# Seven small reorderings and shorter norms in a two-block f32 transformer kernel, with the identity products behind the expert loop taken out

## The reference

```python
def first_block(x, mem, ...):
    h = rmsnorm(x, g_mix)
    proj = h @ w_in                                  # q, k, v, u
    mixed = concat([rmsnorm(sb, g_sb_out), rmsnorm(pooled, g_pool_out)])
    x = x + mixed @ w_out
    x = x + memory_cross_attention(rmsnorm(x, g_mem_q), rmsnorm(mem, g_mem_kv), w_mem_q, w_mem_kv, w_mem_o)
    x = x + moe_ffn(rmsnorm(x, g_ffn), w_router, b_router, w1, b1, w2, b2)   # top 4 of 32, clamped SwiGLU
    return rmsnorm(x, g_final)

def second_block(x, p, ...):
    cols = _rms_norm(x, g_pre) @ w_in                # 1024 -> 6272 columns
    y_a, y_b = attention(...), time_mix(...)
    merged = sigmoid(gate_a) * (y_a @ p_a) + sigmoid(gate_b) * (y_b @ p_b)
    h = x + _rms_norm(merged @ w_out, g_post)
    return h + sigmoid(h @ w_ple_gate) * (p @ w_ple_up)
```

## Time and profile before

| | us |
|---|---|
| median of 3 runs | 1480.3 (1479.57 to 1480.72) |
| the profiled execution | 1479.94 |
| its span, first to last instruction | 1478.1 |
| TensorE busy | 1416.4 (96%) |
| VectorE, ScalarE, GpSimd busy | 485.1, 387.6, 72.0 |
| mean granted clock of TensorE | 0.995 |
| read from HBM | 479.2 MB |

### The profile page before, as it was taken

The page is one execution under the profiler, slowest core; times in us unless marked ns, Lnnn a source line. Parts: engine busy times, 40 slices in busy tenths (PEclk is TensorE's granted clock), DMA queues, the critical chain, the costliest instruction groups (busy, mean ns, idle before and its releaser), DMA issues.

```text
span 1478.1 us, 21334 instructions
## 1 busy us (share of the span) xinstructions
PE 1416.4 (96%) x9123; PEld 765.5 (52%) x9123; DVE 485.1 (33%) x736; ACT 387.6 (26%) x540; POOL 72.0 (5%) x74
## 2 busy tenths in 40 slices
PE   8999999999999999999999999999999899899997
PEld 8898984333333333333333333233333699888686
DVE  5475543112112112111211111112111467875465
ACT  6555532111111111111111111111111556631133
POOL 1220000000000000000000000000000100261000
PEclk9999999999999999999999999999999999999999
DMA  9545378999999999999999999999999545322332
GB/s 362 176 136 164 121 290 352 430 426 428 428 427 429 429 428 428 429 428 430 428 427 430 428 430 427 426 429 428 427 427 426 179 158 194 115 88 88 119 128 96
DMA packets 52532, 481.83 MB, mean 326 GB/s; under 512 B 4784, under 2 KB 10416, under 8 KB 27760
## 3 DMA queue, kind: packets, MB, share of 16 engines
q1 hardware_dynamic: 50400, 474.76, 78.5%
q0 software_dynamic: 1168, 4.48, 1.2%
q10 hardware_dynamic: 896, 1.57, 0.3%
HBM read 479.22 MB, written 1.57 MB: 325 GB/s over the span
## 4 chain that ended last, share of the span: by engine, by line
PE 72%; DMA 21%; ACT 3%; DVE 3%; issue 1%; POOL 0%; SPq 0%; ACTq 0%; DVEq 0%
PE PS L1013 20%; DMA ring<-in_w_expert_in_dram 14%; PE PS L1032 11%; DMA big<-in_w_expert_in_dram 7%; PE PS L719 4%; PE PS L720 4%; PE PS L721 4%; PE PS L1039 3%; PE PS L984 3%; PE PS L725 2%; PE PS L727 2%; PE PS L726 2%; PE PS L1282 2%; PE PS L999 2%; PE PS L1331 2%; PE PS L992 1%
## 5 line engine op out<-in xcount | busy, mean ns | idle before, releaser
L1013 PE MATMUL PS<-ring,big 128*64 128x512 f32 x1536 | 340.9, 595 | 18.4 <-DMA ring<-in_w_expert_in_dram 18.1
L2269 DVE TENSOR_SCALAR big<-PS 128x512 f32<-128x512 f32 x32 | 22.1, 692 | 701.3 <-PE PS L1013 701.3
L1013 PEld LDWEIGHTS PS<-ring,big 128*64 128x64 f32 x1536 | 105.9, 137 | 251.0 <-issue 209.8
L1032 PE MATMUL PS<-ring,big 128*64 128x512 f32 x768 | 170.1, 595 | 0.2 <-ACT big L1739 0.2
L1730 ACT ACTIVATE big<-big 128x512 f32<-128x512 f32 x32 | 20.1, 629 | 479.9 <-DVE big L2269 479.9
L1013 PE MATMUL PS<-big 128*64 128x512 f32 x512 | 116.0, 603 | 5.4 <-DMA big<-in_w_expert_in_dram 5.1
L719 PE MATMUL PS<-uT_high,w_high 128*128 128x256 f32 x352 | 102.9, 292 | 2.3 <-DVE w_rest L2096 1.3
L1032 PEld LDWEIGHTS PS<-ring,big 128*64 128x64 f32 x768 | 53.8, 137 | 99.1 <-issue 97.1
L720 PE MATMUL PS<-uT_rest,w_high 128*128 128x256 f32 x352 | 99.1, 282 | 0.0
L721 PE MATMUL PS<-uT_high,w_rest 128*128 128x256 f32 x352 | 98.4, 280 | 0.0
L1580 ACT ACTIVATE w_high<-ring 128x1024 fp32r<-128x1024 f32 x65 | 68.7, 1059 | 104.6 <-PE PS L721 82.1
(11 more groups left out here) (415 smaller groups left out, 1894.9 us busy)
## 6 DMA issues: line engine op xcount, KB each, us to landing
ring<-in_w_expert_in_dram SPq DMA_DIRECT2D x96, 2048.0 KB, 30.9
ring<-in_w_expert_out_dram SPq DMA_DIRECT2D x48, 2048.0 KB, 34.7
big<-in_w_expert_in_dram SPq DMA_DIRECT2D x32, 2048.0 KB, 30.7
ring<-in_w_in_dram SPq DMA_DIRECT2D x32, 1024.0 KB, 5.1
big<-in_w_expert_out_dram SPq DMA_DIRECT2D x16, 2048.0 KB, 34.1
ring<-in_w_mem_kv_dram SPq DMA_DIRECT2D x8, 1024.0 KB, 5.5
ring<-in_w_out_dram SPq DMA_DIRECT2D x8, 1024.0 KB, 5.0
ring<-in_w_mem_q_dram SPq DMA_DIRECT2D x4, 1024.0 KB, 5.2
```

The source lines that it names most:

```text
L1013: t = mm(PS[CAP * c:CAP * c + CAP, 2 + b, :], xT_e[:, 2 * (j % 2) + i, j // 2, :], w[:, i, D * b + 512 * c:D * b + 512 * c + 512], start=F ...
L1032: t = mm(PS[CAP * c:CAP * c + CAP, 0, :], actT[:, i, n, :], w[:, i, 512 * c:512 * c + 512], start=n + i == 0, stop=n + i == 4)
```

## The change

Eight edits; the first seven are those of the first line, the eighth takes products out.

1. The identity products at the start: 8 calls in place of 16.
2. The scores of the first attention are copied out of PSUM in two parts, by VectorE and ScalarE. Each now has its own semaphore, and TensorE goes on to the memory keys when VectorE's part is done, whose banks it needs.
3. ScalarE and VectorE split the transposed mixer rows (`split_T(2)`) before weight chunk 15 and not after it.
4. VectorE copies the second half of the transposed probabilities before it splits chunk 25.
5. Norm 4: the rows are scaled (`norm_thirds`: half 0 whole, half 1 in two parts of 512 columns, all on VectorE) and transposed (`transpose_thirds`), in place of the scaled identity. ScalarE's scaling of half 1 goes.
6. Norm 6 likewise; ScalarE's scaling of half 1 goes here too.
7. The last unit gets buffers of its own (`W2_high[2]`, `W2_rest[2]` in ring slot 9), so its split waits for no earlier unit, and the last two units run by halves of the tokens: half 0 of both, then half 1 of both.
8. Six places of identity products behind the expert loop go (8 calls before the branch, 5 behind it and 1 behind the transposes; 8 before the second output projection; 11 before and 3 behind the transposes ahead of the last gate). Those before the router stay.

The same replacement of `W2_...[u % 2]` by `W2_...[unit_buf(u)]` in the splits of VectorE and GpSimd is left out here.

```diff
@@ -159,6 +159,8 @@
+        for i, W2 in enumerate((W2_high, W2_rest)):
+            W2.append(nc.alloc_sbuf_tensor_at(f"w2_last{i}", [128, D], f32r, offset=ring_at + 4 * SLOT * 9 + 4 * D * i))
@@ -401,6 +401,7 @@
+        s_z_first = sem("s_z_first")
@@ -538,6 +539,10 @@
+        def unit_buf(u):
+
+            return 2 if u == U_END - 1 else u % 2
+
@@ -690,14 +695,14 @@
-            def turn_scaled(rows, bank, ready, n):
+            def transpose_thirds(rows, bank, ready, n):
...
-                    pe.wait_ge(ready, n + h)
...
-                        t = mm(ps[:, k, 128 * h:128 * h + 128], rows[:, h, 128 * k:128 * k + 128], r_diag[:, h, :],
-                               start=True, stop=True)
+                        if k == 0 or h == 1 and k == 4:
+                            pe.wait_ge(ready, n + h + k // 4)
+                        t = transpose(ps[:, k, 128 * h:128 * h + 128], rows[:, h, 128 * k:128 * k + 128], ident)
@@ -708,7 +713,7 @@
-            stay_busy(6, 16)
+            stay_busy(6, 8)
@@ -869,7 +874,7 @@
-            pe.wait_ge(s_z_copied, 2)
+            pe.wait_ge(s_z_first, 1)
@@ -949,9 +954,8 @@
-            turn_scaled(X, 4, s_norm_rows, 9)
+            transpose_thirds(HN, 4, s_norm_rows, 9)
...
-            pe.wait_ge(s_eye4, 1)
@@ -1045,7 +1049,7 @@
-            pe.wait_ge(s_norm_rows, 12)
+            pe.wait_ge(s_norm_rows, 11)
@@ -1118,9 +1122,6 @@
             scatter_half(1).then_inc(s_scattered, 1)
-            stay_busy(0, 8)
-
-
             with pe.If(over[0] > 0):
@@ -1146,15 +1147,13 @@
-            stay_busy(0, 5)
-            transpose_halves(HN, 0, s_norm_rows, 15)
-            stay_busy(5, 1)
+            transpose_thirds(HN, 0, s_norm_rows, 14)
...
-                return W2_high[u % 2][:, :], W2_rest[u % 2][:, :]
+                return W2_high[unit_buf(u)][:, :], W2_rest[unit_buf(u)][:, :]
@@ -1172,7 +1171,7 @@
-                               W2_high[u % 2][:, 512 * c:512 * c + 512], start=True, stop=False)
+                               W2_high[unit_buf(u)][:, 512 * c:512 * c + 512], start=True, stop=False)
@@ -1498,7 +1497,6 @@
-            stay_busy(4, 8)
             pe.wait_ge(s_e_evac, 1)
@@ -1506,11 +1504,21 @@
-            stay_busy(0, 11)
...
-            stay_busy(4, 3)
-            for k in range(KT):
+            for k in range(KT - 2):
...
+            last = [post_unit(u) for u in (U_END - 2, U_END - 1)]
+            for h in range(TH):
+                ts = slice(128 * h, 128 * h + 128)
+                for k in (KT - 2, KT - 1):
+                    wH, wL = last[k - KT + 2]
+                    xT_tile(7, k)
+                    for c in range(2):
+                        t = split_rows(wH, wL, slice(512 * c, 512 * c + 512), uT[0][:, k, ts], uT[1][:, k, ts],
+                                       PS[:, 4 + 2 * h + c, :], False, k == KT - 1)
+                if h == 0:
+                    t.then_inc(s_part_done, 1)
+            t.then_inc(s_ring_used, 2)
@@ -1575,9 +1583,9 @@
-                if u >= 2:
+                if 2 <= u < U_END - 1:
...
-                fn(W2_high[u % 2][:, :], slot(sl, D * half, D * half + D), ACT.Copy).then_inc(s_w_high, 1)
+                fn(W2_high[unit_buf(u)][:, :], slot(sl, D * half, D * half + D), ACT.Copy).then_inc(s_w_high, 1)
@@ -1636,7 +1644,8 @@
-            act.wait_ge(s_z_copied, 2)
+            act.wait_ge(s_z_first, 1)
+            act.wait_ge(s_z_copied, 1)
@@ -1674,8 +1683,8 @@
             fn(frow[0:HEADS, :], PS[0:HEADS, 7, :], ACT.Copy).then_inc(s_frow_evac, 1)
+            split_T(2, HTH, "g_sb_out")
             split_w(15)
-            split_T(2, HTH, "g_sb_out")
             for n in range(16, 20):
@@ -1714,7 +1723,6 @@
             evac_T(5, 4, HT, "g_ffn")
-            second_half(4)
@@ -1785,9 +1793,8 @@
-                        act.wait_ge(s_norm_rows, 13 + h)
+                        act.wait_ge(s_norm_rows, 12 + h)
...
-            second_half(6)
@@ -2041,10 +2048,10 @@
-            def norm_diag(n):
-                for h in range(TH):
-                    half_rstd(n, h)
-                    v.tensor_scalar(r_diag[:, h, :], ident, stat[:, 32 + 2 * n + h:33 + 2 * n + h], None, ALU.mult)\
+            def norm_thirds(n):
+                norm_rows(n)
+                for c in (slice(0, 512), slice(512, 1024)):
+                    v.tensor_scalar(HN[:, 1, c], X[:, 1, c], stat[:, 33 + 2 * n:34 + 2 * n], None, ALU.mult)\
@@ -2127,13 +2134,13 @@
             dve.wait_ge(s_z_done, 1)
-            v.tensor_copy(Z[:, 0:4, :], PS[:, 4:8, 0:384]).then_inc(s_z_copied, 1)
+            v.tensor_copy(Z[:, 0:4, :], PS[:, 4:8, 0:384]).then_inc(s_z_first, 1)
             split_w(9)
...
                 dve.wait_ge(s_late_loaded, 16)
-                dve.wait_ge(s_z_copied, 2)
+                dve.wait_ge(s_z_copied, 1)
                 dve.wait_ge(s_z_ln, g + 1)
@@ -2173,8 +2180,8 @@
             v.tensor_copy(mv_rows[:, :, 256:512], PS[:, 5, :].rearrange("p (h n) -> p h n", h=TH)).then_inc(s_qkv_evac, 1)
+            split_T(2, HTH, HTL, "g_sb_out")
             split_w(15)
-            split_T(2, HTH, HTL, "g_sb_out")
             for n in range(16, 20):
@@ -2199,20 +2206,19 @@
                     .then_inc(s_p_ready, 1)
-            split_w(25)
             dve.wait_ge(s_tr_p, 2)
             v.tensor_copy(probT[:, 4:8, :], banks(0, 2, S)).then_inc(s_pT_evac, 1)
+            split_w(25)
             split_T(4, HTH, HTL, None)
...
                 split_w(n)
-            v.tensor_reduce(eye4, ident.rearrange("p (g e) -> p e g", e=N_EXP), AX, ALU.add).then_inc(s_eye4, 1)
+            v.tensor_reduce(eye4, ident.rearrange("p (g e) -> p e g", e=N_EXP), AX, ALU.add)
             dve.wait_ge(s_part_done, 2)
...
-            norm_diag(4)
-            v.tensor_scalar(HN[:, 0, :], X[:, 0, :], stat[:, 40:41], None, ALU.mult).then_inc(s_norm_rows, 1)
+            norm_thirds(4)
             dve.wait_ge(s_bias_written, 16)
@@ -2349,7 +2355,7 @@
-            norm_rows(6)
+            norm_thirds(6)
```

8 lines of the change are left out of this document (3 added, 5 removed).

## The result

The changed kernel takes **1481.65 us** (median of 20 runs, 1478.42 to 1484.64), the kernel before 1479.51 (20 runs, 1478.55 to 1480.72): a ratio of 1.0015, 95% interval 1.0009 to 1.0022. It is slower by about 2 us; 1477.4 was forecast, with 1480.4 as the upper end of the range. Its runs also scatter more, over 6.2 us against 2.2.

A forecast was written before the change was run, and what follows sets the result against it. The expert-weight load stream bounds the loop, TensorE mostly the rest. From 1479.94 us, -4.5 ahead of the loop, +0.5 at the branch and +1.0 before the last units give 1476.9; forecast 1477.4, range 1474.8 to 1480.4.

The forecast's parts named there:

- start: Kernel's start: fewer identity instructions let transposes and VectorE's splits come earlier, 1.5 us saved, bounds 1.0 and 1.9.
- scores: Before the memory keys: TensorE starts earlier but then waits for the third chunk's split, 0 saved, bounds 0 and 0.2.
- `split_T(2)`: Around weight chunk 15, 117 us: splitting the transposed rows first nearly removes two TensorE idles, 0.9 us saved, upper bound 1.4.
- chunk 25: Around 187 to 191 us: VectorE's copy of the probabilities no longer waits behind this split, 0.9 us saved.
- norm: Before the router: scaling rows and then transposing starts the router's products earlier, 1.2 us saved, bounds 0.8 and 1.4.
- The rival of swallowed savings: Ahead of the loop: half of the 4.5 us is lost if the first loads set the stream's start; 1479.6, chance 0.23.
- The gaps: Behind the loop, without identity products: +0.5 us at the branch, 0 in the middle, +1.0 before the last eight units.
- if the clock stays low to 1169 or so, some tenths more; to 1172, 1.5 us more: At the branch: extra cost on top of twelve half-clock transposes ending 0.3 us later; term +0.5, bounds -0.85 and +2.
- The upper bound of the middle gap: At the wait ending with ScalarE's copy at 1404 us: 1.7 us lost were the clock to fall; term itself 0.
- less than the 2.48 us that brought the clock down: At the wait ending at 1404 us: TensorE's 2.0 us idle was taken as too short to lower the clock, so 0.
- 1.53 us of idling are left, and the clock holds: Before the last eight units, kernel before: this short idle keeps full clock; without the products, a 4.0 us gap costs +1.0 us.
- Third buffer and halves: Last two units: splits come earlier, but TensorE waits for both before unit 63; end unmoved, 0, bounds -0.3 and +0.5.

The follow-up runs named there:

- the five edits with padding: Kernel before with edits 1 to 5, plus four identity products in each of the last eight experts: 1477.48 us, ratio 0.9979.
- the kernel without the products: Kernel before with its identity products at six places behind the expert loop removed, nothing else changed: 1482.28 us, ratio 1.0015.
- the changed kernel with 32 products: Changed kernel plus four identity products in each of the last eight experts: 1479.38 us, against 1481.98 without them; ratio to the kernel before 0.9995.
- all edits but the products kept and padded: Changed kernel with its products behind the loop put back, plus four in each of the last eight experts: 1477.39 us, ratio 0.9985 to the kernel before.

## Why the prediction was wrong

- **Ahead of the loop: right.** Steps in the trace: start 1.5 (forecast 1.5), scores 0 (0), `split_T(2)` 0.75 (0.9), chunk 25 0.95 (0.9), norm 1.25 (1.2), together 4.5 us at expert 0 and at the loop's end. The rival of swallowed savings is out. What failed is the baseline: the 1.5 us of the start were read off one execution with a late clock; by the means of the traces they are 1.0. In the medians the five edits with padding are worth 2.5 us (interval of the ratio: 1.8 to 4.4). Some 0.4 us of the rest is the code's border in its trace, 0.5 the start; what makes up the remaining microsecond stays open. The clock also falls at 230 to 234 us in three of 17 traces, two of kernels with the old start and one with the five edits, and costs 1.65 us at expert 0 there; no run shows why.
- **The gaps: mechanism right, size too small.** Forecast +0.5, 0 and +1.0; measured +0.82, +0.17, +1.32, and 2.5 for all. The step "if the clock stays low to 1169 or so, some tenths more; to 1172, 1.5 us more" was put as a bound, and it is what the traces of the changed kernel (second) and of the kernel without the products show. The upper bound of the middle gap, 1.7 us, came true in one trace of the changed kernel. The Trainium skill's rule in "TensorE: Matmul & The Clock Gate" (section "HAM oscillation — how this bites in real kernels"), that work behind a long gap starts cold, holds at all twelve gaps of 4.0 and 6.1 us in these traces; here 1.97 us of idling were once enough too, and 1.53 us three times. So two comparisons of the prediction do not stand: "less than the 2.48 us that brought the clock down" (four of eleven traces with that wait at the branch, 2.2 to 2.8 us long, kept the full clock there), and "1.53 us of idling are left, and the clock holds", read off one execution. I took one likely course of the clock for each gap; the right sum is a mean over the courses, with and without the products.
- **The code: missing altogether.** This is the step that failed. The change part by part counted what 208 fewer instructions of TensorE save, not where they leave the rest, and the sum has no term for it. It cost 1.5 and 1.6 us in the two traces and, by the changed kernel with 32 products, 2.6 us in the median. Without it the result would lie within the range. A hint stood in the rows: the earlier trace rows has 2.48 us of idling with "issue" as its releaser, behind a branch. I read it as an empty gap for the clock. It is probably a wait for code as well: every trace in which products follow the branch at once has it (2.2 to 2.8 us), wherever the code lies.
- **Third buffer and halves: right, 0,** with the norm by thirds at 0.4 us in the medians or nothing.
- In sum: -2.5 (front) + 0.4 + 2.5 (products) + 1.8 (code, the part seen in the traces and outside the span) = +2.2 us; measured +2.1 and +2.2. Forecast: -2.9. The first three terms have intervals of over 1 us to either side, so that the sum comes out to a tenth is luck.

## What to carry over

A deleted instruction moves all the code behind it. Where a program has runs of tiny products, compare TensorE's waits with the releaser "issue" before and after, and shift the code with a few instructions in a wait that is long enough, before a difference of 0.1% is put down to the edit. Count the shift in the trace and not in the source: one call was four instructions here, and my padding went 64 instructions past its aim. Identity products in a gap buy clock behind the gap; remove them last, and count the gap's cost over several executions, never from one trace. And take a term that depends on the clock's timing, such as the start, from several traces of the same kernel.

## What the runs showed of the hardware

- TensorE waits up to 0.8 us at a block's border, every 256th instruction, where products of 17 ns follow each other, and 0.3 to 1.1 us are lost there in all. No packet of the instruction queue is in flight meanwhile: the wait ends 1.3 to 1.6 us after the last one's end. What the engine does in that time no run shows. That it simply ran dry is doubtful, since in the kernel before no such packet moves from 436 to 925 us, while the loop runs some 4500 instructions, over 1000 to a turn. The Trainium skill's "Runtime: NRT & Kernel Launch" (section "Instruction fetch mechanics") says that code streams in blocks of 256 instructions and that a taken branch can force a load before execution goes on; the traces agree (waits a multiple of 256 instructions apart, packets of 16 KB; 2.2 to 2.8 us behind the branch, ending 1.5 to 1.7 us after a packet's end). It also says that the cost of a block's border is mostly hidden; with dense tiny products it was not.
- Two kernels, the changed one (both times) and the one with all edits but the products kept and padded, had runs that lasted 2.4 to 3.0 us longer than their span where all others have 1.8. Shifting the code removed it in the changed kernel and brought it out in the other. That the end of the program crosses a block's border there is a guess; it was not tried.
- The start of kernels that are alike up to the loop moves by up to 1.5 us between executions; the 32 products take 5.44 to 6.57 us, with the moment at which TensorE's clock rises.
